# The last output chunk of three down projections computed one stream at a time, with the next norm and panel folded in

## The reference

```
u  = rmsnorm(h) * A[stream] + B[stream]          # A, B per feature, from the conditioning vector
h  = h + gate[stream] * (silu(u Wg) * (u Wu)) Wd # "up" then "down"
u' = rmsnorm(h) * A'[stream] + B'[stream]        # then the next product: u' W_in, or u' Wg, u' Wu
```

## Time and profile before

| | |
|---|---|
| median of 3 runs | 2383.7 us (2381.66 to 2384.02) |
| the profiled execution | 2387.36 us, its span 2386.1 us |
| mean granted TensorE clock | 0.979 |
| TensorE busy | 2279.2 us, 96% |
| VectorE busy | 1497.5 us, 63% |
| ScalarE busy | 959.8 us, 40% |

### The profile page before, as it was taken

How to read it: one execution, slowest core, us unless ns; L and a number is a source line. 1 busy time by engine, 2 the same in 40 slices (tenths; PEclk the granted TensorE clock), 3 DMA queues, 4 the chain that set the end, 5 groups by cost and what they waited for, 6 DMA issues and landing times. The chain is left out here.

```text
span 2386.1 us, 37057 instructions
## 1 busy us (share of the span) xinstructions
PE 2279.2 (96%) x14376; PEld 1925.4 (81%) x14376; DVE 1497.5 (63%) x2306; ACT 959.8 (40%) x1540; POOL 368.1 (15%) x365
## 2 busy tenths in 40 slices
PE   6999999998999999999999999879999999998998
PEld 4888887765678888878888876669998998798998
DVE  4666766545775666676664346466667766676874
ACT  4222223454542222242222245444446434555763
POOL 1000001000000000000000010039995476000000
PEclk9999999999999999999999999989999999999999
DMA  7554444111134444434443241114544332234544
GB/s 281 185 188 175 172 167 168 71 36 53 54 128 163 168 178 161 167 136 159 174 177 121 97 141 54 70 58 156 191 170 151 114 108 72 88 135 157 187 168 149
DMA packets 52615, 331.05 MB, mean 139 GB/s; under 512 B 6544, under 2 KB 7824, under 8 KB 21648
## 3 DMA queue, kind: packets, MB, share of 16 engines
q1 hardware_dynamic: 49040, 319.15, 37.0%
q0 software_dynamic: 3456, 10.25, 1.4%
HBM read 325.56 MB, written 3.80 MB: 138 GB/s over the span
## 5 line engine op out<-in xcount | busy, mean ns | idle before, releaser
L1181 PE MATMUL bank<-u_hi,whi 128*128 128x512 f32 (+1 forms) x2512 | 865.2, 344 | 29.2 <-DVE u_lo L1135 13.6
L1182 PE MATMUL bank<-u_lo,whi 128*128 128x512 f32 (+1 forms) x2512 | 849.8, 338 | 0.0
L1183 PE MATMUL bank<-u_hi,wlo 128*128 128x512 f32 (+1 forms) x2512 | 849.2, 338 | 0.0
L568 DVE TENSOR_TENSOR wlo<-raw,whi 128x2048 fp32r<-128x2048 f32 (+2 forms) x207 | 434.9, 2101 | 314.9 <-ACT whi L566 314.8
L1181 PEld LDWEIGHTS bank<-u_hi,whi 128*128 128x128 f32 x2512 | 477.3, 190 | 104.7 <-issue 30.3
L1183 PEld LDWEIGHTS bank<-u_hi,wlo 128*128 128x128 f32 x2512 | 477.4, 190 | 52.1
L1182 PEld LDWEIGHTS bank<-u_lo,whi 128*128 128x128 f32 x2512 | 477.5, 190 | 49.5 <-issue 0.2
L566 ACT ACTIVATE whi<-raw 128x2048 fp32r<-128x2048 f32 (+2 forms) x207 | 353.1, 1706 | 338.5 <-PE bank L1183 234.1
L1243 ACT ACTIVATE sil<-bank 128x512 f32<-128x512 f32 (+1 forms) x88 | 48.0, 545 | 543.6 <-PE bank L1183 543.5
L1181 PE MATMUL bank<-hidden_hi,whi 128*128 128x512 f32 x528 | 205.4, 389 | 0.0
L1182 PE MATMUL bank<-hidden_lo,whi 128*128 128x512 f32 x528 | 205.4, 389 | 0.0
(11 more groups left out here) (426 smaller groups left out, 2938.7 us busy)
## 6 DMA issues: line engine op xcount, KB each, us to landing
raw<-in_stream SPq DMA_DIRECT2D x231, 1024.0 KB, 4.8
raw<-in_stream SPq DMA_DIRECT2D x80, 704.0 KB, 4.0
first_ada<-in_stream SPq DMA_DIRECT2D x8, 1024.0 KB, 16.5
raw<-in_stream SPq DMA_DIRECT2D x8, 768.0 KB, 4.4
skew<-rpb_rows POOLq DMA_DIRECT2D x8, 336.0 KB, 6.1
nbr_bias<-skew POOLq DMA_DIRECT2D x24, 112.0 KB, 3.5
h<-in_tokens SPq DMA_DIRECT2D x1, 2048.0 KB, 11.6
uq_ukv<-in_small POOLq DMA_DIRECT2D x1, 1536.0 KB, 8.1
```

The lines of the kernel that those rows point to most:

```text
L568: v.tensor_tensor(self.lo[to][:, 0:n], raw[:, 0:n], self.hi[to][:, 0:n].bitcast(F32), ALU.subtract).then_inc(self.s_lo, 1)
L1181: pe.q.matmul(dst, w[0], x[0], start=start, stop=False)
L1182: pe.q.matmul(dst, w[0], x[1], start=False, stop=False)
L1183: return pe.q.matmul(dst, w[1], x[0], start=False, stop=stop)
```

## The change

In the down stages that are followed by a norm of two streams (down1 of both layers, down2 of layer 0), `run` stops before the last group (`last_left`), and `last_group_by_stream` does that group and the first panel of the next stage in an order of its own. Both are done for the first stream (`x = 0`) and then for the second, with matmuls of 256 columns. The first panel of the next stage is split in two halves (`split_chunks`: chunks 0 to 3 and 4 to 7), now between the steps of the norm. The norm has five steps for each stream: chunk 0, chunk 1 (slim), chunks 2 and 3, 4 and 5, 6 and 7 (wide, two chunks of one stream). The second panel's quarters (`split_hi`, `split_lo`) stand between the second stream's steps. `("in", 1)` computes its query tile for the first stream alone, as before.

```diff
@@ Stream @@
+    def split_chunks(self, ph, x):
+
+        a, v, g = self.e.A, self.e.V, ph.first
+        slot, to = self.slot["own"][g], g % 2
+        raw, hi, lo = [t[:, :].rearrange("p (b n) -> p b n", b=2)[:, :, SLAB // 4 * x:SLAB // 4 * x + SLAB // 4]
+                       for t in (self.raw[slot], self.hi[to], self.lo[to])]
+
+        def high():
+            if x == 0:
+                a.q.wait_ge(self.s_raw[slot], self.there["own"][g])
+                a.q.wait_ge(self.s_pe, g - 1)
+                self.first_chunks = a.do(a.q.activation(hi, raw, ACT.Copy))
+            else:
+                a.q.activation(hi, raw, ACT.Copy).then_inc(self.s_hi, 1)
+
+        def low():
+            if x == 0:
+                v.after(self.first_chunks)
+                return v.do(v.q.tensor_tensor(lo, raw, hi.bitcast(F32), ALU.subtract))
+            v.q.wait_ge(self.s_hi, g + 1)
+            v.q.tensor_tensor(lo, raw, hi.bitcast(F32), ALU.subtract).then_inc(self.s_lo, 1)
+
+        return high, low
...
-            for m in range(2 + body * rounds, n_groups):
+            for m in range(2 + body * rounds, n_groups - last_left):
...
+        if last_left:
+            self.groups += n_groups
+            return
...
@@ gate_up: the first panel's multiply is begun()[1] @@
@@ down @@
+        st.run(name, multiply, evacuate, ppg=2, early=True, middle=square, last_left=bool(staged))
         sq_count[0] += KC - 1
+        if staged:
+            G, first_panel = st.groups - 1, PHASE[name].first
+            evacuate(Count(KC - 2), 1 - G % 2, Count(G - 1), Count(first_panel + 14))
+            st.split(PHASE[name], Count(15))
+            square(Count(KC - 2), 1 - G % 2, Count(G - 1))
+            return last_group_by_stream(name, gates, hidden, then, *staged)
...
@@ new function @@
+    def last_group_by_stream(name, gates, hidden, then, coeff, dst, both):
+        ph, nx, G = PHASE[name], PHASE[then], st.groups - 1
+        m, out_bank, panel = KC - 1, 2 * (G % 2), ph.first + 14
+        square_to, product_to = prod[sq_count[0] % 2], prod[1 - sq_count[0] % 2]
+        cols = [slice(x * S, x * S + S) for x in range(2)]
+        def half(x, part, tiles_):
+            for t in tiles_:
+                kc = part * 11 + t
+                r = three(banks[out_bank + x][:, 0:S], tile_of((panel + part) % 2, t), chunk_of(hidden, kc, x * S, x * S + S),
+                          kc == 0, kc == FC - 1)
+            return r
+        def final_residual(x):
+            return dve.q.scalar_tensor_tensor(out=h[:, m, cols[x]], in0=banks[out_bank + x][:, 0:S], scalar=gates(Count(m), x),
+                                              in1=h[:, m, cols[x]], op0=ALU.mult, op1=ALU.add)
+        def final_square(x):
+            return act.do(act.q.activation(square_to[:, cols[x]], h[:, m, cols[x]], ACT.Square))
+        def sums(x, squared):
+            pe.after((s_ss, sq_count[0]))
+            for src in (ssq, square_to):
+                if src is square_to:
+                    pe.after(squared)
+                for t in range(2):
+                    r = pe.q.matmul(banks[4 + x][:, t:t + 1], src[:, x * S + t * P:x * S + (t + 1) * P], cst("ones", 1),
+                                    start=src is ssq and t == 0, stop=src is square_to and t == 1)
+            return pe.do(r)
+        def inverse(x, summed):
+            act.after(summed)
+            r = act.do(act.q.activation(inv[:, x, :], banks[4 + x][:, 0:2], ACT.Sqrt, scale=1.0 / D, bias=cst("eps", 1)))
+            dve.after(r)
+            dve.after(dve.do(dve.q.reciprocal(inv[:, x, :], inv[:, x, :])))
+            return dve.do(dve.q.tensor_tensor(
+                diag[:, cols[x]].rearrange("p (t q) -> p t q", q=P),
+                cst("ident").rearrange("p (o q) -> p o q", o=1).to_broadcast([P, 2, P]),
+                inv[:, x, :].rearrange("p (t o) -> p t o", o=1).to_broadcast([P, 2, P]), ALU.mult))
+        def spread_out(x, mark):
+            pe.after(mark)
+            spread[x] = pe.do(pe.q.matmul(banks[4 + x][:, 0:S], cst("ones"), diag[:, cols[x]], start=True, stop=True))
+        steps = [(x, cs) for x in range(2) for cs in ((0,), (1,), (2, 3), (4, 5), (6, 7))]
+        spread, ready = [None, None], [[None] * KC, [None] * KC]
+        multiplied, high_done, step_done, product_read = {}, {}, {}, [None]
+        def chunks(t, i):
+            x, cs = steps[i]
+            return t[:, cs[0], cols[x]] if len(cs) == 1 else t[:, cs[0]:cs[1] + 1, cols[x]]
+        def scaled_to(i):
+            to = sil[i % 2]
+            return to[:, 0:S] if len(steps[i][1]) == 1 else to[:, :].rearrange("p (a t) -> p a t", a=2)
+        def multiply_step(i):
+            x, cs = steps[i]
+            factor = banks[4 + x][:, 0:S]
+            if len(cs) == 1:
+                dve.after(spread[x], step_done.get(i - 2))
+                r = dve.q.scalar_tensor_tensor(out=scaled_to(i), in0=chunks(h, i), scalar=coeff(cs[0], x)[0], in1=factor,
+                                               op0=ALU.mult, op1=ALU.mult)
+            else:
+                dve.after(spread[x], product_read[0])
+                r = dve.q.tensor_tensor(product_to[:, :].rearrange("p (a t) -> p a t", a=2), chunks(h, i),
+                                        factor.rearrange("p (o t) -> p o t", o=1).to_broadcast([P, 2, S]), ALU.mult)
+            multiplied[i] = dve.do(r)
+        def high_step(i):
+            x, cs = steps[i]
+            act.after(multiplied[i], step_done.get(i - 2))
+            if len(cs) == 1:
+                high_done[i] = act.do(act.q.activation(chunks(u_hi, i), scaled_to(i), ACT.Identity, bias=coeff(cs[0], x)[1]))
+                return
+            for k, c in enumerate(cs):
+                A, B = coeff(c, x)
+                r = act.do(act.q.activation(sil[i % 2][:, k * S:k * S + S], product_to[:, k * S:k * S + S], ACT.Identity,
+                                            scale=A, bias=B))
+            product_read[0] = r
+            act.after(r)
+            high_done[i] = act.do(act.q.activation(chunks(u_hi, i), scaled_to(i), ACT.Copy))
+        def low_step(i):
+            x, cs = steps[i]
+            dve.after(high_done[i])
+            high = chunks(u_hi, i).bitcast(F32)
+            if len(cs) == 1:
+                r = dve.q.scalar_tensor_tensor(out=chunks(u_lo, i), in0=scaled_to(i), scalar=coeff(cs[0], x)[1], in1=high,
+                                               op0=ALU.add, op1=ALU.subtract)
+            else:
+                r = dve.q.tensor_tensor(chunks(u_lo, i), scaled_to(i), high, ALU.subtract)
+            step_done[i] = dve.do(r)
+            for c in cs:
+                ready[x][c] = step_done[i]
+        def next_panel(x, kc):
+            pe.after(ready[x][kc])
+            for b in range(2):
+                if x == 0 or both[b]:
+                    r = three(dst[b][:, cols[x]], tile_of(nx.first % 2, b * KC + kc), chunk_of(u, kc, x * S, x * S + S),
+                              kc == 0, kc == KC - 1)
+                    if b == 0 and kc == KC - 1 and x == both[0]:
+                        tile_done[0] = pe.do(r)
+            return r
+        tile_done = [None]
+        (high_a, low_a), (high_b, low_b) = st.split_chunks(nx, 0), st.split_chunks(nx, 1)
+        dve.after(mods_ready[0])
+        act.after(mods_ready[0])
+        pe.q.wait_ge(st.s_lo, panel + 1)
+        pe.q.wait_ge(st.s_ev, G - 1)
+        half(0, 0, range(11))
+        pe.q.wait_ge(st.s_lo, panel + 2)
+        x_done = pe.do(half(0, 1, range(11)))
+        dve.after(x_done)
+        x_added = dve.do(final_residual(0))
+        act.q.wait_ge(s_ss, sq_count[0] - 1)
+        act.after(x_added)
+        squared = final_square(0)
+        half(1, 0, range(4))
+        summed = sums(0, squared)
+        inverted = inverse(0, summed)
+        half(1, 0, range(4, 9))
+        spread_out(0, inverted)
+        half(1, 0, range(9, 11)).then_inc(st.s_pe, 1)
+        half(1, 1, range(11)).then_inc(st.s_pe, 1)
+        for i in range(2):
+            multiply_step(i)
+            high_step(i)
+        for i in range(2):
+            low_step(i)
+        multiply_step(2)
+        high_a()
+        high_step(2)
+        part_ready = low_a()
+        low_step(2)
+        high_b()
+        dve.q.wait_ge(st.s_pe, ph.first + 16)
+        final_residual(1).then_inc(st.s_ev, 1)
+        multiply_step(3)
+        low_b()
+        act.q.wait_ge(st.s_ev, G + 1)
+        squared = final_square(1)
+        high_step(3)
+        low_step(3)
+        pe.after(part_ready)
+        pe.q.wait_ge(st.s_ev, G)
+        for kc in range(3):
+            next_panel(0, kc)
+        summed = sums(1, squared)
+        inverted = inverse(1, summed)
+        multiply_step(4)
+        high_step(4)
+        next_panel(0, 3)
+        pe.q.wait_ge(st.s_lo, nx.first + 1)
+        for kc in (4, 5):
+            next_panel(0, kc)
+        spread_out(1, inverted)
+        low_step(4)
+        st.split_hi(nx, 1, 0)
+        for i in (5, 6):
```

(51 more changed lines are left out.)

## The result

The changed kernel takes 2401.46 us (median of 5 runs, 2398.81 to 2404.71) against 2384.02 for the kernel before on the same chip: ratio 1.0065, 95% interval 1.0047 to 1.0083, so 11 to 20 us slower. The forecast was 2401.7. The profiled execution spans 2403.0 us, 16.9 more than before.

The account below looks back on a forecast made before the run. The chain through VectorE and ScalarE, from the norm's factor to the last chunk, was taken to bound these stretches. 2387.36 + 12.0 (chain) + 6.0 (clock) = 2405.4, less 3.7 for the median: 2401.7 us, range 2392 to 2408.5.

Parts of the forecast that it names:

- The head: Last group to the norm's first multiplication: 12.95 us after the group's start, giving the chain 6.1 us of lead.
- new wait of 0.15: In the first place's last group, TensorE waits 0.15 us for the second panel's low part, with the hand-off.
- The body: VectorE's norm steps: wide steps cost 3.1 us, 3.72 with a quarter; places +4.3, +4.6, +3.1, sum +12.0 us.
- one every 1.65 us: Reading of the old norm on VectorE and ScalarE: its chunks leave at this pace.
- Edits at nothing: First panel's split in waits of steps 2 and 3, third panel's load, POOL's tables, `mod_scales`, roots table: no cost.
- The clock: TensorE's lower clock level reaching the second panel: bounds 0 and 4.2 us a place, taken 2.0, +6.0 in sum.
- by that rule all three places pay: Reading of the Trainium skill: bursts parted by waits start throttled in every place; sum +18 us.
- 2387.36 + 18: Forecast sum for the profiled execution: 2387.36 + 12.0 + 6.0 = 2405.4 us; the median 3.7 lower.
- The winning rival: VectorE's waits in the steps close and TensorE is the bound: 2365.8 us; chance 0.07 closed, 0.06 partly closed.
- point of decision: The winning rival decides where a wide step with its quarter costs under 2.5 us instead of 3.7.
- the rival's half case: Half of the winning rival's effect on VectorE's waits: no change, 2383 us; chance of partly closed waits 0.06.
- The full case: All of VectorE's waits close, TensorE bounds the three places: -5.1, -4.5, -8.3 us, 2365.8; chance 0.07.

Follow-up runs that it names:

- e4_first_only: The change in the first place alone, the two other places as in the kernel before: 2393.27 us, ratio 1.0029 to the kernel before.
- e1_swap: The changed kernel with VectorE's next multiplication ahead of the previous step's subtraction, from the second stream's chunk 1 on: 2386.27 us, ratio 0.9995 to the kernel before.
- e2_warm: The changed kernel with 12 unread matmuls of 256 columns ahead of the second stream's chunks 2, 4 and 6: 2397.5 us, ratio 1.0041 to the kernel before.
- e7_thin_split: The changed kernel with the next stage's first panel split over only 64 of 1024 columns in each half: 2399.25 us, ratio 1.0057 to the kernel before.
- e5_best: The changed kernel with e1_swap's order and four smaller edits to the norm's steps, quarters, spreading and last matmuls: 2382.66 us, ratio 0.9983 to the kernel before.

## Why the prediction was right

- *The head.* The first multiplication came 12.7 us after the last group's start (399.51 - 386.79; forecast 12.95): the lead of some 6 us is real. The "new wait of 0.15" was 0.06 in this execution (12.66 in the other two places, 12.8 forecast), but it is no constant: 0.3 in e4_first_only, 0.65 in e1_swap's first place, and the 1.2 us of e2_warm show what a late load makes of it.
- *The body.* Forecast was that the order of VectorE's queue makes each wide step pay its whole way round, 3.12 us and 3.72 with a quarter; measured 3.11 and 3.71, of which 1.82 is wait (forecast 1.9). The last subtraction ended 142.6 us after the down start, and with the 0.59 us by which this execution began later taken off, at 424.1, forecast 424.4. The three places cost 4.0, 4.6 and 3.0 us by the chain (second panels' starts, less 1.1 and 0.6 for a last burst at half pace), 11.6 in sum; forecast 4.3, 4.6, 3.1, in sum 12.0. e1_swap shows the cause by taking away that order. One reading was too smooth: "one every 1.65 us" holds within a pair of wide chunks, while from pair to pair the old norm took 5.36 us for three chunks (409.04 and 414.40), 1.8 a chunk. The sum doesn't use it.
- *Edits at nothing.* e7_thin_split shows it for the split. e4_first_only shows that nothing is passed on from place to place. The loads and tables of the in stage were not varied by a run; behind the second panel the first place takes 165.5 us to attention's output projection, 166.0 before, so no cost of theirs is to be seen.
- *The clock.* Taken were 2.0 a place between bounds of 0 and 4.2. The trace has 2.6, 1.7 and 2.1, in sum 6.4 for 6.0, and e2_warm gives back 5.7 by the ratios. The sum was right and taking the middle was luck in part: e4_first_only has a place with the very same pattern and no fall, e7_thin_split's second place too, and in its first a fall of 3.4 us from 418.5 on lies in the bursts and costs nothing at the second panel. What the Trainium skill says (TensorE: Matmul & The Clock Gate, section "HAM oscillation — how this bites in real kernels") holds here as a tendency: between the bursts lie waits of 1.5 to 2.4 us in the first place, up to 3.1 in the third, and in the profiled execution there is a fall in each place; not every execution follows it. That section's own example has longer waits, for DMA, so "by that rule all three places pay" took it further than it goes.
- *Where it was off.* The 2387.36 + 18 of the profiled execution would be 2405.4; it was 2403.0 + 1.3 = 2404.3. The ratio says +15.5 us (11 to 20). That 18.1 us are lost in the three places and 16.9 in the span was not forecast. And that the median, 2401.46, is within 0.3 us of the 2401.7 is luck: the medians of the kernel before alone lie 3 us apart from set to set (2384.0, 2387.0, 2386.2).
- *The winning rival* was named with a point of decision, a round under 2.5 us, and that point was set too high: e1_swap reaches 1.84 to 2.18 and stands only at no change, where the rival's half case had been put (2383 forecast for it; 0.9995 measured). The swap shortens the second stream's steps alone; steps 2 and 3 of the first stream still go 3.1 us round. The full case, TensorE as the bound, was not reached by e5_best either: its TensorE still waits in front of chunks, 0.93 and 1.14 us in the first place.

## What to carry to other kernels

When a chain goes back and forth between two in-order queues, write the next item's first step ahead of this item's last one; check it by looking for one wait of equal length in front of the same line, round after round. Starting a chain 6 us earlier is worth nothing if each of its links waits for the other engine. Before a stage is put into bursts, ask which dense stage follows them, for it is there that a lower clock is paid.

## What was not expected of the hardware

- The same sequence of matmuls and waits, alike to 0.1 us, met the lower clock level in one execution (from 426.1, for 6.8 us, in the changed kernel) and not in another (e4_first_only, at 1.00 throughout).
- With matmuls that nobody reads in TensorE's waits the granted clock stayed up in five places of six: 14 a place in the old kernel, where the fall stayed in the third, worth 0.8, 0.0 and 0.0 us; 36 a place in the changed one, worth 5.7 us in all by the ratios. One execution of each was traced.
- A load of 704 KB took 6.05 us once where its neighbours took 4, which was enough to delay a place by 1.2 us.
